# A two-layer hybrid encoder with a hierarchical mixture of experts: row gathers in two halves on 128 partitions

## The chip, the cores and the metric

The kernel runs on one core of a Trainium2 chip. The metric is the device time of one execution in microseconds; less is better. The core has a TensorE (matmuls and weight loads), a VectorE (DVE), a ScalarE (ACT), a GpSimd (POOL), a SyncE (SP), and 16 DMA engines that move data between DRAM and the on-chip memory (SBUF, 128 partitions). The matmuls write into PSUM.

## The reference

All numbers are fp32. 544 tokens (512 of a prompt and 32 of a running stream) of 1024 features pass through two layers. Each layer has a token mixer (A: sliding-window attention with sinks, B: differential attention), a residual add, and a mixture of experts. The change touches the mixture of experts, which reads, shortened:

```python
def hier_moe(h, ...):                      # h: rms_norm of the residual rows
    g_idx  = argmax(softmax(x @ w_rg + b_rg))          # 1 of 4 groups
    top_v, top_i = top_k(softmax(el of that group), 2) # 2 of its 8 experts
    gate   = g_prob * top_v / sum(top_v)               # 0 for all other experts
    for g in range(4):                                 # 32 experts in all
        a  = einsum('nd,edf->nef', x, w_gate[g])       # 1024 -> 256
        u  = einsum('nd,edf->nef', x, w_up[g])         # 1024 -> 256
        hh = silu(a) * u * gate[:, g, :, None]
        y  = y + einsum('nef,efd->nd', hh, w_down[g])  # 256 -> 1024
```

Each token goes to two of 32 experts. An expert has three matrices of 1 MB, so a layer reads 96 MB of expert weights.

## The kernel before

**Stages.** Layer 0's projections and attention are followed by its expert stage (about 256 to 494 us of the trace), then come layer 1's projections and attention, and its expert stage (about 893 to 1140). Tokens lie in five tiles (four of 128 rows, one of 32).

**Rows to experts.** After a tile's attention output is added, POOL writes the tile's residual rows to a scratch in DRAM, `hn_scratch`, one row of 4 KB per token (`rows_out`, L601). The router gives each token and choice an expert and a rank within it; an expert has `CAP` = 64 places. The rank of the token that stands in place s is a number in the constant table `C_SLOT`. A chain of matmuls against these tables makes, for each expert, a list that holds in place s the key of a token and choice; key = `KEY0` - 2 x token - choice. DVE turns keys into two lists of indices in `idx_i` (L1423 to L1426): the token, for the gather, and the half row of the output, for the scatter. The output scratch `y_scratch` (in the code `y2_dram`) holds 2 KB half rows, four per token: two choices by two halves.

**One expert.** In the profile a tensor `area` is the big SBUF buffer from which all tiles below are cut.

- POOL gathers (L667): an indirect DMA of up to 64 rows of 4 KB into `xg[e % 4]`. Even experts use partitions 0 to 63 and odd ones 64 to 127, each with 1024 columns.
- TensorE turns the rows (`x_transpose`, L2055): 8 transposes of 64 rows by 128 columns into one PSUM bank, so that features lie on partitions.
- DVE multiplies by the norm's gains on the way to SBUF (`scale_x`, L1463).
- TensorE multiplies by gate and up (`gate_up`, L2071 and L2072): 8 steps, each a pair that writes partitions 0 to 63 (gate) and 64 to 127 (up) of PSUM.
- ACT takes silu (L964), and DVE multiplies with up and the token's factor (L1469).
- TensorE transposes the result (`h_transpose`, L2077: two transposes of 64 by 128), DVE copies it (L1477), and TensorE multiplies by the down matrix (`down`, L2083 and L2084).
- DVE copies y (L1484), and POOL scatters 128 half rows of 2 KB (L673).

**Order.** TensorE's order is written out by hand: for each e, `gate_up(e)`, `x_transpose(e+1)`, `down(e-1)`, `h_transpose(e)`. POOL issues the first four gathers of a layer at once, and gather e+4 as soon as `x_transpose(e)` is done; scatters and gathers share its queue. SP issues the weight loads (L511) of 1 MB each in the order in which TensorE reads them (gate and up of e, then down of e-1) into 21 slots; a load waits for the last use of its slot. The down matrix is read as `(c p) d`: partition p holds rows p and 128 + p, two runs of 4 KB in DRAM. The gate and up matrices have one run of 8 KB per partition.

**A block beyond 64 rows.** When an expert has more than 64 rows, the rest goes through the same steps as an extra block after expert 21 (`overfull_rows`, with a chain of `STEPS` = 11 small DVE steps that makes its list in `ov_i`, and `overfull_expert` on TensorE). In layer 0 no expert has one; in layer 1 one expert with 72 rows does.

Late in the expert stage SP also reads the residual rows of four tiles back into `hid` (L550), whose space held weights meanwhile.

## Time and profile before

| | us |
|---|---|
| median of 3 runs | 1176.37 |
| lowest and highest of them | 1175.69, 1179.66 |
| profiled execution, its own time | 1176.92 |
| its span in the trace | 1175.0 |
| TensorE busy (PE) | 1037.6 |
| TensorE's weight loads (PEld, beside PE) | 738.9 |
| VectorE busy | 421.3 |
| GpSimd busy | 282.9 |
| ScalarE busy | 231.9 |

The profile's page divides the span into 40 slices of 29.4 us; each digit is a busy share in tenths, `PEclk` the granted TensorE clock in tenths of full speed, and `GB/s` what the 16 DMA engines moved. The expert stages are the two stretches at 370 to 403 GB/s (slices 10 to 17 and 32 to 39):

```
PE   6999999969999887939899899899999997999889970
PEclk9999999979999999959999999999997999999995
DMA  9312043559999999984320302145176999999996
GB/s 312 112 41 105 8 173 149 192 187 390 371 379 383 377 378 387 403 311 150 108 84 28 127 30 91 64 175 203 41 287 257 385 382 379 376 386 402 376 380 235
```

A busy TensorE is not one at its peak, and a matmul that waits for an operand is not counted as busy; a wait is put down to what came last.

### The profile page before, as it was taken

The page shows a single profiled execution, that of the slowest core. Times are in us where ns is not written, and L with a number is a line of the kernel's source. Part 1 is how long each engine was busy: PE and PEld are TensorE (multiplying, and loading weights), DVE is VectorE, ACT ScalarE, POOL GpSimd, SP SyncE. Part 2 cuts the span into 40 slices and gives each one's busy share as a digit, 9 for nine tenths or more (in the row PEclk, how much of TensorE's full clock was granted, in tenths as well). Part 3 has the DMA queues.
Part 4 walks back from the last instruction along what each step waited for, and adds up shares of the span by engine and source line. Part 5 has one row for each costly group of instructions (what it writes and reads, how often), then busy time and mean ns, then how long its engine had stood idle before and what let it go on. Part 6 is the DMA issues. An engine that isn't in the chain of part 4 may idle for free.

```text
span 1175.0 us, 18007 instructions
## 1 busy us (share of the span) xinstructions
PE 1037.6 (88%) x6864; PEld 738.9 (63%) x6864; DVE 421.3 (36%) x1365; ACT 231.9 (20%) x717; POOL 282.9 (24%) x440
## 2 busy tenths in 40 slices
PE   6999999969999887939899899999997999889970
PEld 6877778955555444528667687777884555555540
DVE  1234454333233222251242533435563333332326
ACT  4234441010000000023122333323310000000001
POOL 3612231022322222122021221221202223221213
PEclk9999999979999999959999999999997999999995
DMA  9312043559999999984320302145176999999996
GB/s 312 112 41 105 8 173 149 192 187 390 371 379 383 377 378 387 403 311 150 108 84 28 127 30 91 64 175 203 41 287 257 385 382 379 376 386 402 376 380 235
DMA packets 82168, 282.17 MB, mean 240 GB/s; under 512 B 10102, under 2 KB 36806, under 8 KB 64352
## 3 DMA queue, kind: packets, MB, share of 16 engines
q1 hardware_dynamic: 65840, 240.40, 54.7%
q0 software_dynamic: 14992, 31.66, 8.3%
q10 hardware_dynamic: 1248, 8.91, 2.0%
q8 instruction: 58, 0.95, 0.3%
q14 instruction: 30, 0.25, 0.1%
HBM read 268.66 MB, written 28.70 MB: 253 GB/s over the span
## 4 chain that ended last, share of the span: by engine, by line
PE 72%; DMA 15%; DVE 4%; SPq 3%; issue 2%; ACT 2%; POOL 1%; ACTq 0%; POOLq 0%; DVEq 0%
PE ps L1767 22%; PE ps L2071 14%; PE ps L1759 10%; DMA area<-in_w_up 9%; PE ps L2083 6%; PE ps L2055 4%; SPq L511 3%; DMA area<-in_w_down 3%; PE ps L2261 2%; PE ps L1743 2%; PE ps L1830 1%; PE ps L1952 1%; PE ps L2227 1%; PE ps L1967 1%; PE ps L1982 1%
## 5 line engine op out<-in xcount | busy, mean ns | idle before, releaser
L1767 PE MATMUL ps<-area 128*128 128x256 f32 x1152 | 267.8, 385 | 7.6 <-DMA area<-in_w_b_qkv 3.9
L2072 PE MATMUL ps<-area 128*64 128x256 f32 x1040 | 252.7, 399 | 0.0
L2071 PE MATMUL ps<-area 128*64 128x256 f32 x912 | 221.6, 399 | 30.2 <-DMA area<-in_w_up 20.3
L1767 PEld LDWEIGHTS ps<-area 128*128 128x128 f32 x1152 | 215.2, 192 | 38.7 <-issue 8.8
L2071 PEld LDWEIGHTS ps<-area 128*64 128x64 f32 x912 | 126.1, 143 | 92.7 <-issue 35.5
L673 POOL DMA_INDIRECT y_scratch<-area,idx_i x64 | 64.8, 1013 | 360.3 <-DVE area L1484 319.7
L2072 PEld LDWEIGHTS ps<-area 128*64 128x64 f32 x1040 | 143.4, 143 | 0.0
L1759 PE MATMUL ps<-area 128*128 128x272 f32 x512 | 123.2, 395 | 0.0
L1469 DVE SCALAR_TENSOR_TENSOR area<-ps,area 64x256 f32<-64x256 f32 x64 | 31.4, 491 | 246.2 <-ACT area L964 246.2
L964 ACT ACTIVATE area<-ps,area 64x256 f32<-64x256 f32 x64 | 29.9, 468 | 449.6 <-PE ps L2072 449.6
L2083 PE MATMUL ps<-area 128*64 128x512 f32 x228 | 109.9, 604 | 1.2 <-DVE area L1477 0.8
L2084 PE MATMUL ps<-area 128*64 128x512 f32 x228 | 109.9, 604 | 0.0
L1759 PEld LDWEIGHTS ps<-area 128*128 128x128 f32 x512 | 95.0, 190 | 18.9 <-issue 0.6
L929 ACT ACTIVATE area<-area,small 128x256 f32<-128x256 f32 (+5 forms) x160 | 80.2, 502 | 87.1 <-DVE small L1230 87.1
L2055 PEld LDWEIGHTS ps<-cst,area 64*128 64x128 f32 x512 | 61.3, 201 | 34.6 <-issue 29.3
L2055 PE MATMUL ps<-cst,area 64*128 64x64 f32 x512 | 70.1, 278 | 10.4 <-DMA area<-hn_scratch,idx_i 10.4
L1223 DVE CUSTOM_DVE_ANT_0 area<-ps,area 128x256 f32<-128x256 f32 (+5 forms) x160 | 59.1, 423 | 44.9 <-PE ps L1952 25.2
L667 POOL DMA_INDIRECT area<-hn_scratch,idx_i x64 | 61.3, 958 | 39.4 <-issue 19.9
L791 POOL TENSOR_SCALAR area<-area,small 32x288 f32<-32x288 f32 (+4 forms) x40 | 20.5, 521 | 162.0 <-DVE small L1655 162.0
L658 POOL TENSOR_SCALAR area<-area,small 128x256 f32<-128x256 f32 (+2 forms) x80 | 33.7, 439 | 92.5 <-DVE small L1258 92.5
L2083 PEld LDWEIGHTS ps<-area 128*64 128x64 f32 x228 | 26.7, 136 | 37.7 <-issue 32.4
L1477 DVE COPY area<-ps 128x128 f32<-128x128 f32 x64 | 18.6, 291 | 88.1 <-PE ps L2077 88.1
(235 smaller groups left out, 1157.1 us busy)
## 6 DMA issues: line engine op xcount, KB each, us to landing
area<-in_w_up SPq DMA_DIRECT2D x65, 1024.0 KB, 25.5
area<-in_w_gate SPq DMA_DIRECT2D x57, 1024.0 KB, 25.2
area<-in_w_down SPq DMA_DIRECT2D x57, 1024.0 KB, 25.6
area<-in_w_b_qkv SPq DMA_DIRECT2D x12, 1024.0 KB, 8.5
hid<-in_w_down SPq DMA_DIRECT2D x8, 1024.0 KB, 26.3
hid<-in_w_gate SPq DMA_DIRECT2D x8, 1024.0 KB, 26.6
area<-y_scratch ACTq DMA_DIRECT2D x8, 1024.0 KB, 8.1
area<-in_w_a_qkv SPq DMA_DIRECT2D x6, 1024.0 KB, 13.0
```

What stands on the lines that cost most here:

```text
L511: sp.dma_start(dst.rearrange("p (k f) -> p k f", f=src.shape[-1]), src).then_inc(landed, 16)
L667: nc.gpsimd.indirect_dma_start(xg[e % XG], None, hn_dram, bass.IndirectOffsetOnAxis(ap=idx_i[0:CAP, 1, e:e + 1], axis=0), bounds_check=N - ...
L673: nc.gpsimd.indirect_dma_start(y2_dram, bass.IndirectOffsetOnAxis(ap=idx_i[:, 0, e:e + 1], axis=0), yout[e % 2], None, bounds_check=4 * N ...
L929: ins = nc.scalar.activation(E[:r, g, 0:nk], E[:r, g, 0:nk], ACT.Exp, bias=sm[:r, 4 + g:5 + g], scale=SCALE, accum_out=sm[:r, 8 + g:9 + g])
L1223: ins = nc.vector.tensor_tensor_reduce(out=E[:r, g, 0:nk], in0=ps[:r, b, c:c + nk], in1=tab(j, g)[:r, tc:tc + nk], scale=1.0, scalar=-3e38 ...
L1759: ins = nc.tensor.matmul(ps[:, bank, 0:HALF_N], w[:, k, m * P:m * P + P], x[:, k, HALF_N * h:HALF_N * h + HALF_N], start=k == 0, stop=k == ...
L1767: ins = nc.tensor.matmul(ps[:r, bank, at_col:at_col + F], x[:, k, COL[t]:COL[t] + r], w[:, k, :], start=k == k0, stop=k == k1 - 1)
L2055: ins = nc.tensor.transpose(ps[:, 2 + b, k * CAP:k * CAP + CAP], x[:, k, :], ident[lo:lo + CAP, lo:lo + CAP])
L2071: nc.tensor.matmul(ps[0:CAP, bank, 0:F], x[:, k, :], wg[:, k, :], start=k == 0, stop=k == KD - 1)
L2072: ins = nc.tensor.matmul(ps[CAP:P, bank, 0:F], x[:, k, :], wu[:, k, :], start=k == 0, stop=k == KD - 1)
L2083: nc.tensor.matmul(ps[0:CAP, bank, :], ht[:, c, :], wd[:, c, 0:OUT_HALF], start=c == 0, stop=c == 1)
L2084: ins = nc.tensor.matmul(ps[CAP:P, bank, :], ht[:, c, :], wd[:, c, OUT_HALF:D], start=c == 0, stop=c == 1)
```

## The change

The edits, which belong together:

- `hn_scratch` becomes an array of 2 KB half rows like the output scratch, and each token's row stands in it twice, once for each of its two choices (`residual_rows`; `rows_out` writes both copies in one DMA of 1 MB per tile, and the read back of the residual takes the first).
- So one index, 4 x token + 2 x choice + half, serves gather and scatter. `C_HALF` now carries 2 x `KEY0` + half, and one DVE instruction makes the list in place of four. In the overfull block three chained steps fall away (`STEPS` 11 to 8).
- A gather takes 128 half rows of 2 KB: the first halves of the rows on partitions 0 to 63, the second halves on 64 to 127, into `xg` tiles of 512 columns.
- TensorE turns them by `turn_rows`: 4 x 2 x 2 = 16 matmuls of 64 by 64 against the identity in place of 8 transposes; the two of a pair read partitions 0 to 63 and 64 to 127 and write the same partitions of one PSUM bank.
- Feature 512 h + 8 c + k of a row thus lands on partition 64 h + c in step k, where it was before; gate and up weights and the gains are as they were.
- The down matrix is read as `(p c) d`, one run of 8 KB per partition, and `expert_ht` reads the gated rows with every second column to match.
- `C_SLOT`, the table of places: of the 64 places, counted s, s // 4 % 8 is a group of four partitions and s % 4 + 4 (s // 32) a turn; ranks go round the eight groups, one row to each, back and forth. Before, they went in quarters of 16.
- The y tile of the overfull block moves to make room.

```diff
--- before.py
+++ after.py
@@ -85,14 +85,14 @@
     c[:, C_K2:C_K2 + NT] = KEY0 - 2 * tok - 1
     c[:, C_BY1:C_BY1 + NT] = 1.0 / c[:, C_K1:C_K1 + NT]
     c[:, C_BY2:C_BY2 + NT] = 1.0 / c[:, C_K2:C_K2 + NT]
-    c[:, C_HALF] = np.arange(P) // CAP
+    c[:, C_HALF] = 2 * KEY0 + np.arange(P) // CAP
     c[:, C_THR:C_THR + 8] = CAP * np.arange(1, 9)
     c[:, C_IOTA:C_IOTA + NE] = np.arange(NE)
 
 
-    u, v, b = np.arange(CAP) // 16, np.arange(CAP) // 4 % 4, np.arange(CAP) % 4
-    quarter, at = (u + b) % 4, 4 * v + u
-    c[:, C_SLOT:C_SLOT + CAP] = 16 * quarter + np.where(quarter % 2 == 0, at, 15 - at)
+    s = np.arange(CAP)
+    group, turn = s // 4 % 8, s % 4 + 4 * (s // 32)
+    c[:, C_SLOT:C_SLOT + CAP] = 8 * turn + np.where(turn % 2 == 0, group, 7 - group)
     c[:, C_BEFORE:C_BEFORE + P] = np.arange(P)[:, None] < np.arange(P)[None, :]
     c[:, C_ONE:C_ONE + P] = 1.0
     q = np.arange(P)[:, None]
@@ -228,7 +228,7 @@
     def sem(name):
         return ctx.enter_context(nc.semaphore(name))
 
-    hn_dram = nc.dram_tensor("hn_scratch", [N, D], F32).ap()
+    hn_dram = nc.dram_tensor("hn_scratch", [4 * N, OUT_HALF], F32).ap()
     y2_dram = nc.dram_tensor("y2_scratch", [4 * N, OUT_HALF], F32).ap()
 
 
@@ -312,13 +312,13 @@
     junk = [part(norm_at[n] + 3 * D if n in norm_at else R_G, D) for n in range(5)]
 
 
-    xg = [part(D * (i // 2), D)[CAP * (i % 2):CAP * (i % 2) + CAP, :] for i in range(XG)]
-    xg_extra = part(R_G, D)[0:CAP, :]
+    xg = [part(OUT_HALF * i, OUT_HALF) for i in range(XG)]
+    xg_extra = part(R_G, OUT_HALF)
     M1 = XG // 2 * D
     xts = [part(M1 + 512 * i, KD, CAP) for i in range(2)]
     sil = [part(M1 + 1024 + 256 * i, F) for i in range(2)]
     hts = [part(M1 + 1536 + 128 * i, 2, CAP) for i in range(2)]
-    yout = [part(M1 + 1792 + 512 * i, OUT_HALF) for i in range(2)] + [part(R_G, OUT_HALF)]
+    yout = [part(M1 + 1792 + 512 * i, OUT_HALF) for i in range(2)] + [part(R_G + OUT_HALF, OUT_HALF)]
     assert M1 + 1792 + 2 * 512 <= slot_at["W0"] and slot_at["W0"] + SLOT <= M0
     ovw = part(R_R + 4 * SLOT, 3, SLOT)
     y2b = [part(2 * D * i, 2, D) for i in range(3)] + [part(R_X + 2 * D * i, 2, D) for i in range(2)]
@@ -347,7 +347,7 @@
     root = part(M0 + 3000, NE)
     assert M0 + 3000 + NE <= R_G
     first_of = sb("first_of", [P, NT, 2, 8], U32)
-    idx_i = sb("idx_i", [P, 3, NE], I32)
+    idx_i = sb("idx_i", [P, NE], I32)
     ov_i = sb("ov_i", [P, 8], I32)
     ov_u = sb("ov_u", [1, 8], U32)
 
@@ -481,6 +481,10 @@
 
         return at["ab"[layer], "o"], NT * (k_end // 2 - 1) + LATE.index(t) + 1
 
+    def residual_rows(t):
+
+        return hn_dram[4 * COL[t]:4 * COL[t] + 4 * ROWS[t], :].rearrange("(p c h) d -> p c (h d)", c=2, h=2)
+
     block = ctx.enter_context(nc.Block())
 
 
@@ -494,7 +498,7 @@
 
         gate = [I["w_gate"][l].rearrange("g e (p k) f -> (g e) p k f", k=KD) for l in range(2)]
         up = [I["w_up"][l].rearrange("g e (p k) f -> (g e) p k f", k=KD) for l in range(2)]
-        down = [I["w_down"][l].rearrange("g e (c p) d -> (g e) p c d", p=P) for l in range(2)]
+        down = [I["w_down"][l].rearrange("g e (p c) d -> (g e) p c d", p=P) for l in range(2)]
 
         def source(key):
             kind, x, i = key[0], key[1], key[2]
@@ -547,7 +551,7 @@
             for name in ("H1", "H0"):
                 sp.wait_ge(*last_use([key for key, at in MOE_LOADS[layer] if at == name][-1]))
                 for t in (2 * int(name[1]), 2 * int(name[1]) + 1):
-                    sp.dma_start(hid[:, t, :], hn_dram[COL[t]:COL[t] + P, :]).then_inc(tile_in[t], 16)
+                    sp.dma_start(hid[:, t, :], residual_rows(t)[:, 0, :]).then_inc(tile_in[t], 16)
 
             with sp.If(extra > 1):
                 with sp.Fori(1, extra) as o:
@@ -598,7 +602,7 @@
             t = TILES[n][i]
             r = ROWS[t]
             pool.wait_ge(hid_attn, OUT_DONE[n // 2][t])
-            pool.dma_start(hn_dram[COL[t]:COL[t] + r, :], hid[:r, t, :]).then_inc(y_out[i % 2], 16)
+            pool.dma_start(residual_rows(t), hid[:r, t, :].unsqueeze(1).broadcast_to([r, 2, D])).then_inc(y_out[i % 2], 16)
 
         def g_load():
             pool.dma_start(gbc, I["norm_final"].rearrange("(o d) -> o d", o=1).broadcast_to([P, D])).then_inc(g_in, 16)
@@ -665,20 +669,20 @@
 
             def gather(e):
                 nc.gpsimd.indirect_dma_start(xg[e % XG], None, hn_dram,
-                                             bass.IndirectOffsetOnAxis(ap=idx_i[0:CAP, 1, e:e + 1], axis=0),
-                                             bounds_check=N - 1, oob_is_err=False).then_inc(gath[e % XG], 16)
+                                             bass.IndirectOffsetOnAxis(ap=idx_i[:, e:e + 1], axis=0),
+                                             bounds_check=4 * N - 1, oob_is_err=False).then_inc(gath[e % XG], 16)
 
             def scatter(e):
                 wait_apart(pool, ye_sb, NE * layer + e + 1)
-                nc.gpsimd.indirect_dma_start(y2_dram, bass.IndirectOffsetOnAxis(ap=idx_i[:, 0, e:e + 1], axis=0),
+                nc.gpsimd.indirect_dma_start(y2_dram, bass.IndirectOffsetOnAxis(ap=idx_i[:, e:e + 1], axis=0),
                                              yout[e % 2], None, bounds_check=4 * N - 1, oob_is_err=False) \
                     .then_inc(scat[e % 2], 16)
 
             def overfull_gather(o, x):
                 wait_apart(pool, s["idx"], o + 1)
                 nc.gpsimd.indirect_dma_start(x, None, hn_dram,
-                                             bass.IndirectOffsetOnAxis(ap=ov_i[0:CAP, 4:5], axis=0),
-                                             bounds_check=N - 1, oob_is_err=False).then_inc(s["gath"], 16)
+                                             bass.IndirectOffsetOnAxis(ap=ov_i[:, 5:6], axis=0),
+                                             bounds_check=4 * N - 1, oob_is_err=False).then_inc(s["gath"], 16)
 
             def overfull_scatter(o):
                 wait_apart(pool, s["y"], o + 1)
@@ -689,10 +693,9 @@
             pool.wait_ge(at["ab"[layer], "o"], UNITS)
             for b in range(2):
                 pool.wait_ge(y_out[b], 16 * (3, 2)[b] * (layer + 1))
-            wait_apart(pool, r_idx, 2 * layer + 1)
+            wait_apart(pool, r_idx, layer + 1)
             for e in range(XG):
                 gather(e)
-            pool.wait_ge(r_idx, 2 * layer + 2)
             for e in range(NE):
                 if e + XG < NE:
                     wait_apart(pool, x_flip, NE * layer + e + 1)
@@ -1420,10 +1423,7 @@
 
             cnt = ovs[0:1, 0:NE]
             dve.wait_ge(r_slots, layer + 1)
-            own(dve, nc.vector.tensor_scalar(idx_i[:, 2, :], ps[:, 3, 0:NE], -1.0, float(KEY0), ALU.mult, ALU.add))
-            nc.vector.tensor_scalar(idx_i[:, 1, :], idx_i[:, 2, :], 1, None, ALU.arith_shift_right).then_inc(r_idx, 1)
-            own(dve, nc.vector.tensor_scalar(em[:, 0, :], ps[:, 3, 0:NE], -2.0, float(2 * KEY0), ALU.mult, ALU.add))
-            nc.vector.tensor_scalar(idx_i[:, 0, :], em[:, 0, :], cst[:, C_HALF:C_HALF + 1], None, ALU.add) \
+            nc.vector.tensor_scalar(idx_i[:, :], ps[:, 3, 0:NE], -2.0, cst[:, C_HALF:C_HALF + 1], ALU.mult, ALU.add) \
                 .then_inc(r_idx, 1)
 
             def per_tile(i):
@@ -1483,7 +1483,7 @@
                     dve.wait_ge(scat[b], 16 * (NE // 2 * layer + e // 2))
                 nc.vector.tensor_copy(yout[b], ps[:, 6 + b, :]).then_inc(ye_sb, 1)
 
-            STEPS = 11
+            STEPS = 8
             k = [0]
 
             def link(o, ins):
@@ -1529,10 +1529,7 @@
                 link(o, nc.vector.tensor_tensor_reduce(
                     out=blocks[:, 64:64 + NE], in0=ps[:, 3, NE:2 * NE], in1=blocks[:, 0:NE], scale=1.0, scalar=0.0,
                     op0=ALU.mult, op1=ALU.add, accum_out=ovs[:, 117:118]))
-                link(o, nc.vector.tensor_scalar(ov_i[:, 6:7], ovs[:, 115:116], -1.0, float(KEY0), ALU.mult, ALU.add))
-                link(o, nc.vector.tensor_scalar(ovs[:, 116:117], ovs[:, 115:116], -2.0, float(2 * KEY0), ALU.mult, ALU.add))
-                link(o, nc.vector.tensor_scalar(ov_i[:, 5:6], ovs[:, 116:117], cst[:, C_HALF:C_HALF + 1], None, ALU.add))
-                nc.vector.tensor_scalar(ov_i[:, 4:5], ov_i[:, 6:7], 1, None, ALU.arith_shift_right) \
+                nc.vector.tensor_scalar(ov_i[:, 5:6], ovs[:, 115:116], -2.0, cst[:, C_HALF:C_HALF + 1], ALU.mult, ALU.add) \
                     .then_inc(s["idx"], 1)
                 assert k[0] == STEPS, k
 
@@ -2049,12 +2046,16 @@
                     pe.wait_ge(s["count"], layer + 1)
                 if e >= 2 or layer:
                     wait_apart(pe, x_sb, NE * layer + e - 1)
-                x = xg[e % XG].rearrange("p (c k) -> p k c", k=KD)
-                lo = CAP * (e % 2)
+                turn_rows(xg[e % XG], 2 + b).then_inc(x_flip, 1)
+
+            def turn_rows(rows, bank):
+
+                x = rows.rearrange("p (c k) -> p k c", k=KD)
                 for k in range(KD):
-                    ins = nc.tensor.transpose(ps[:, 2 + b, k * CAP:k * CAP + CAP], x[:, k, :],
-                                              ident[lo:lo + CAP, lo:lo + CAP])
-                ins.then_inc(x_flip, 1)
+                    for lo in (0, CAP):
+                        ins = nc.tensor.matmul(ps[lo:lo + CAP, bank, k * CAP:k * CAP + CAP], x[lo:lo + CAP, k, :],
+                                               ident[lo:lo + CAP, lo:lo + CAP], start=True, stop=True)
+                return ins
 
             def gate_up(e):
 
@@ -2073,9 +2074,9 @@
                 return ins
 
             def expert_ht(h, bank):
+                rows = h[CAP:P, :].rearrange("s (p c) -> s c p", c=2)
                 for c in range(2):
-                    ins = nc.tensor.transpose(ps[:, bank, c * CAP:c * CAP + CAP], h[CAP:P, c * P:c * P + P],
-                                              ident[CAP:P, CAP:P])
+                    ins = nc.tensor.transpose(ps[:, bank, c * CAP:c * CAP + CAP], rows[:, c, :], ident[CAP:P, CAP:P])
                 return ins
 
             def expert_down(ht, wd, bank):
@@ -2116,10 +2117,7 @@
 
             def overfull_expert(o, rows):
                 wait_apart(pe, s["gath"], 16 * (o + 1))
-                x = rows.rearrange("p (c k) -> p k c", k=KD)
-                for k in range(KD):
-                    ins = nc.tensor.transpose(ps[:, 3, k * CAP:k * CAP + CAP], x[:, k, :], ident[0:CAP, 0:CAP])
-                ins.then_inc(s["xf"], 1)
+                turn_rows(rows, 3).then_inc(s["xf"], 1)
                 pe.wait_ge(s["xs"], o + 1)
                 pe.wait_ge(s["w"], 48 * (o + 1))
                 wv = ovw[:, :, :].rearrange("p j (k f) -> p j k f", f=F)
```

The order of the instructions on TensorE stays; in one expert's round, from the second half of `gate_up(e)` to the first of `gate_up(e+1)`, the turn has other instructions. Before, on TensorE, layer 0 (`cst` holds the identity; `...` leaves out the rest of `down`):

```order
L2072 MATMUL ps<-area 64x256
L2055 MATMUL ps<-cst,area 128x64 x8
L2083 MATMUL ps<-area 64x512
L2084 MATMUL ps<-area 64x512
...
L2077 MATMUL ps<-cst,area 128x64 x2
L2071 MATMUL ps<-area 64x256
```

The same place in the changed kernel, on TensorE:

```order
L2073 MATMUL ps<-area 64x256
L2056 MATMUL ps<-cst,area 64x64 x16
L2084 MATMUL ps<-area 64x512
L2085 MATMUL ps<-area 64x512
...
L2079 MATMUL ps<-cst,area 128x64 x2
L2072 MATMUL ps<-area 64x256
```

Nothing moved in its place: eight transposes of 128 by 64 became sixteen matmuls of 64 by 64, and the lines are one or two further down.

On POOL, at the end of a layer's attention and the start of its expert stage, before (the first two rows are small router steps, L601 is the write of a tile's rows, L667 a gather, L673 a scatter):

```order
L592 TENSOR_SCALAR small<-small 128x1
L593 TENSOR_TENSOR small<-small 128x1
L601 DMA hn_scratch<-hid 128x1024
L667 DMA area<-hn_scratch,idx_i 64x1024 x5
L673 DMA y_scratch<-area,idx_i 2176x512
L667 DMA area<-hn_scratch,idx_i 64x1024
```

And in the changed kernel, on POOL:

```order
L596 TENSOR_SCALAR small<-small 128x1
L597 TENSOR_TENSOR small<-small 128x1
L605 DMA hn_scratch<-hid 256x1x1024
L671 DMA area<-hn_scratch,idx_i 128x512 x5
L677 DMA y_scratch<-area,idx_i 2176x512
L671 DMA area<-hn_scratch,idx_i 128x512
```

Again nothing moved: the write has twice the rows and the gathers have 128 pieces of 512 columns.

## Rows read from the trace of the kernel before

**Rows 1.** Windows, layer 0's expert stage: us; busy PE, PEld, DVE, ACT, POOL; clock; DMA; GB/s

```profile
256.50:384.00 127.50, 126.11 (x930) 72.74 (x932) 37.29 (x72) 8.42 (x18) 33.94 (x36) 0.98 1.02 375
384.00:493.80 109.80, 90.30 (x626) 55.22 (x623) 26.93 (x52) 6.07 (x13) 23.18 (x24) 0.95 1.02 387
```

**Rows 2.** Chain of waits in that stage: start, duration, engine and line

```profile
265.88 0.43 PE ps L2071
...
303.36 1.03 PE ps L2055 x8
...
310.12 1.02 PE ps L2055 x8
...
493.75 0.40 PE ps L2071
```

**Rows 3.** Waits of TensorE, 256 to 505: total us, times, longest

```profile
PE ps L2071 <- DMA area<-in_w_up: 19.5, 12, 3.0
```

**Rows 4.** Windows of two us, and one after the last gather

```profile
353.00:355.00 2.00, 2.00 (x18) 1.05 (x16) 0.89 (x2) 0.00 (x0) 0.00 (x0) 1.00 0.99 408
355.00:357.00 2.00, 2.00 (x22) 1.35 (x20) 0.00 (x0) 0.00 (x0) 1.04 (x2) 1.00 1.06 307
...
360.00:362.00 2.00, 2.00 (x18) 1.22 (x18) 0.89 (x2) 0.00 (x0) 0.00 (x0) 1.00 1.04 424
362.00:364.00 2.00, 2.00 (x22) 1.19 (x18) 0.00 (x0) 0.00 (x0) 1.27 (x2) 1.00 1.04 309
...
476.00:490.00 14.00, 12.70 (x96) 7.85 (x93) 3.39 (x7) 0.78 (x2) 2.03 (x2) 1.00 1.02 413
```

**Rows 5.** POOL's timeline (start, duration), and DMA issues (median us to landing)

```profile
350.21 0.95 POOL L667 DMA_INDIRECT area<-hn_scratch,idx_i  x1 [0.30 <-issue]
...
area<-hn_scratch,idx_i POOLq DMA_INDIRECT x64, 7.7
```

**Rows 6.** DMA queues, 857 to 863, then 847 to 853: packets, MB, share

```profile
q1 hardware_dynamic: 413, 2.58, 102.4%
...
q0 software_dynamic: 167, 0.62, 25.6%
```

**Rows 7.** TensorE's timeline, then groups of weight loads by form (busy, mean ns)

```profile
86.91 1.09 PE L1967 MATMUL ps<-area 128*64 128x128 f32 x16
...
306.72 0.38 PE L2071 MATMUL ps<-hid,area 128*64 128x256 f32 x1
...
306.93 0.38 PE L2071 MATMUL ps<-hid,area 128*64 128x256 f32 x1
...
L2055 PEld LDWEIGHTS ps<-cst,area 64*128 64x128 f32 x512 | 61.3, 201 | 34.6 <-issue 29.3 <-DMA area<-hn_scratch,idx_i 5.3
L2077 PEld LDWEIGHTS ps<-cst,area 64*128 64x128 f32 x130 | 12.8, 137 | 52.5 <-issue 52.2 <-DVE area L1469 0.2
```

**Rows 8.** POOL's timeline ahead of layer 1's expert stage

```profile
875.48 0.60 POOL L601 DMA_DIRECT2D hn_scratch<-hid  x1 [20.08 <-DVE hid L1247]
...
887.40 1.24 POOL L667 DMA_INDIRECT area<-hn_scratch,idx_i  x1 [10.12 <-DVE idx_i L1426]
```

**Rows 9.** Layer 1's expert stage: TensorE's waits 980 to 1150, chain, window

```profile
PE ps L2071 <- DMA area<-in_w_up: 4.6, 3, 3.2
PE ps L2071 <- DMA area<-in_w_down: 2.5, 1, 2.5
PE ps L2071 <- DVE ov_i L1535: 2.4, 1, 2.4
...
1084.33 1.02 PE ps L2055 x8
...
1130.95 1.03 PE ps L2055 x8
...
1056.00:1062.00 6.00, 6.00 (x32) 3.50 (x31) 0.00 (x0) 0.00 (x0) 0.00 (x0) 0.58 1.03 394
```

## The prediction

> **What bounds the kernel now.** I read the windows first, then the waits of the expert stage, then the chain there, and last the DMA rate in pieces of two microseconds. The reader is to see which of two suppliers is late: TensorE, or the DMA that brings 3 MB of weights per expert. In layer 0's expert stage the DMA engines are busy all the time, at 375 and 387 GB/s [rows 1]. TensorE goes at its own pace at first: from one turn of gathered rows to the next it takes 6.76 us, 303.36 to 310.12 [rows 2]. Weights come in more slowly than that, the stock of 21 slots runs down, and the last third of the stage waits: 19.5 us in 12 waits, all for a weight load [rows 3]. So the last expert starts at 493.75. At TensorE's own pace it would start at 265.88 + 30 x 6.76 = 468.7 [rows 2]. This stage is bound by the DMA, with 25.05 us to be had before TensorE binds.
>
> Why is the DMA at 381 on average? It is not even. In each expert's 6.8 us there is a quiet part at 408 or 424 GB/s and a dip to 307 or 309; after the last gather there are no dips, and the rate is 413 with scatters still running [rows 4]. A gather issued at 350.21 lands 7.7 us later in the median, so at about 357.9: the dip of 355 to 357 is its data [rows 4, 5]. A scatter moves as many bytes, from 128 partitions, and lies in the quiet part. The gather writes into 64 partitions only. That is the difference on which I build.
>
> **The change part by part.** *Gathers over 128 partitions.* The same bytes arrive as 128 pieces of 2 KB instead of 64 of 4 KB. The sum: layer 0 moves 127.5 x 375 + 109.8 x 387 = 90.3 MB from 256.5 to 493.8 [rows 1]. At 413 GB/s, the rate without gathers [rows 4], that takes 218.6 us and ends at 475.1. The ends of this price: nothing (493.8, if the dips stay) and 424 GB/s (469.5). I take 413, because the scatter is the nearest row to the new gather: 2 KB pieces, 128 partitions, no dip.
>
> *The table of places* sets which partition a row falls into. It adds no instruction. Whether the 16 DMA engines get more equal shares no row shows; I take it at nothing, and the spread of the rate holds it.
>
> *Down weights by 8 KB runs.* One run per partition instead of two of 4 KB. Traffic that is mostly 8 KB pieces cost 102.4% of 16 engines for 6 us and 2.58 MB, 38.1 engine-us per MB; pieces of 4 KB alone 25.6% for 6 us and 0.62 MB, 39.6 [rows 6]. The difference of 1.5 on some 27 loads of 1.05 MB is 42 engine-us, over 16 engines 2.7 us a layer. The lower end is nothing. I take 2.7: the supply of layer 0 ends at 472.4.
>
> *TensorE turns the rows by 16 matmuls of 64x64 in place of 8 transposes of 64x128.* Eight transposes take 1.03 [rows 2]. An ordinary fp32 matmul stands in the trace as two passes, a transpose as one, so 16 matmuls are 32 passes, or 16 steps if the two halves of the array (the pairs at partitions 0 and 64) work at the same time. Pairs on two column halves do that: a pair step with 256 moving columns takes 306.93 - 306.72 = 0.21, and eight pair steps with 128 columns 1.09 in all, 0.13 or less each [rows 7]. With 64 columns I expect a quarter of the first, 0.054 (an estimate from these rows); 16 steps are then 0.86, with the start and the switch of shape about 1.0, the same as now. The ends: 0.86 and, at 0.13 a step, 2.1. I take no change, as the time went with the columns in both rows. If the halves go in turn it is a rival, below.
>
> *Transposes of the gated rows read every second column.* Loading a strided operand takes 201 ns and a dense one of the same size 137 [rows 7]. Two per expert: 0 to 0.13 us. I take 0.065, for the first of the two, since the second loads beside it. Over a layer that is 2.0 us of TensorE's pace, so layer 0's floor goes from 468.7 to 470.7. The DMA's 472.4 is later and decides: **layer 0 gains 493.75 - 472.4 = 21.3 us.**
>
> *Layer 1* has the same stage plus one block for an expert with more than 64 rows, and the DMA is nearly its equal, so TensorE's own work soon binds there. Six experts lie between the turns at 1084.33 and 1130.95: 46.62 us where 6 x 6.76 = 40.56 would do, so 6.1 goes with the weight waits [rows 9]. The block's weights are waited for 2.5 us; I count 1.6, because DVE must still scale the block's freshly turned rows [rows 9]. The block's list costs a wait of 2.4 on DVE, in which three of six chained steps fall away: 0.9 [rows 9]. After the wait for the block's weights its matmuls ran at a granted clock of 0.58, that is at the lower of the two levels for most of 6 us [rows 9]; if the wait goes, up to 2.6 us come back, and I count half. The strided transposes take 33 x 0.065 = 2.1. **Layer 1 gains 6.1 + 1.6 + 0.9 + 1.3 - 2.1 = 7.8 us.** With full clock it is 9.1, without it and without the block's terms 4.0.
>
> *Hidden edits.* The row scratch in DRAM is written twice, 1 MB per tile where it was 512 KB. 4 KB pieces cost 39.6 engine-us per MB [rows 6], so 1.3 us more for a tile. The last write of layer 1 is issued at 875.48 and the first gather waits until 887.40 for its list of indices [rows 8]: 11.9 us of cover. If it were gone, 1.3 us a layer. On POOL, which issues these writes, the gathers and the scatters in one queue, a gather costs 0.95 [rows 5]; even at twice that, one gather and one scatter fit in 6.76. DVE makes the indices in one instruction instead of four, ahead of the first gather: one of about 0.2 us goes from the path, which I do not count. Reading back the residual takes the same pieces at twice the step, in a part of the stage when its slots are no longer needed.
>
> **The sum.** 21.3 + 7.8 = 29.1. The profiled execution took 1176.92, 1.92 more than its span of 1175.0, and 0.55 above the median of 1176.37. 1176.92 - 29.1 = 1147.8; against the median **1147.3**.
>
> **The rivals.** *A, the two halves of the array go in turn.* Then a turn is 32 steps of about 0.055, 1.76, and with start about 0.8 above now. Layer 0's last expert starts at 265.88 + 0.8 + 30 x (6.76 + 0.065 + 0.8) = 495.4, 1.7 later than before, and TensorE binds from the first expert; layer 1 pays 33 x 0.865 = 28.5 and gets 9.9: 18.6 later. Together 20.3 slower: **1196.7**. It decides from 34.95 / 64 = 0.55 us per expert and turn on. For it speaks that no row shows two pairs that differ in rows and columns at once and write the same PSUM bank; against it, that pairs in two column halves do overlap [rows 7]. The Trainium skill, TensorEngine Tiling (Array Packing), section Restrictions and Gotchas, says that different row tiles cannot access the same PSUM bank simultaneously; the new pairs are different row tiles in one bank, on different partitions. No run here shows it yet; by that rule the time would be this rival's, by the rows above the forecast.
>
> *B, the dips belong to gathers as such* (their scattered reads), and spreading the destination changes nothing. Then 2.7 of layer 0 and about 1 of layer 1 remain: **1173**. Against it: the scatter is as scattered on the DRAM side and makes no dip [rows 4].
>
> *C, half of the dip stays.* The rate is 397, between 381 and 413: 90.3 / 397 = 227.5, the end 484.0 - 2.7 = 481.3, a gain of 12.4, and some 5 in layer 1: **1159**.
>
> **How the numbers follow.** The forecast has 0.64, with its own range of 1139 (full clock, 424 GB/s, a turn at 0.86) to 1155; C has 0.12, B 0.09, A 0.15. From 1139 to 1173 lie the forecast, C and B, 0.85 in all, and A is left out. About 0.3% is what a measurement of this kernel can tell from no change: 1172.8 to 1179.9. Faster by more: 0.64 + 0.12 and a little of B, 0.78; within: the rest of B, 0.07; slower: A, 0.15.
>
> **What would show it.** In the windows of the changed kernel the dips are gone and the stage runs at 410 GB/s or more; the turn's line on TensorE takes 1.0 per expert and the spacing stays near 6.8; the waits for weights shrink from 19.5 us in layer 0 to under 3; the last expert of layer 0 starts near 472. Spacing of 7.6 from the first expert on means A; dips of 300 GB/s mean B. The forecast is wrong if the turn costs over half a microsecond more, or if the DMA rate does not rise.

## The result: slower, and the profile after

The changed kernel takes 1217.16 us in the median of five runs (1215.6 to 1218.01), against 1176.93 for the kernel before in the same comparison: a ratio of 1.0335 with a 95% interval of 1.0319 to 1.0351. I had forecast 1147.3, in a range of 1139 to 1173. The profiled execution's span is 1215.0, against 1175.0 before.

The line of the page that shares the chain of work that ended last among the engines now reads, for the changed kernel:

```profile
PE 88%; DVE 4%; DMA 3%; issue 2%; ACT 2%; POOL 1%; ACTq 0%; SPq 0%; POOLq 0%; DVEq 0%
```

Before, the DMA had 15% of this chain, the weight loads above all. Now it has 3%, and TensorE is the bound nearly everywhere. The windows say why the DMA left the chain. Those of layer 0's expert stage in the changed kernel (columns as in [rows 1]), the whole stretch first, then pieces of two us:

```profile
256.50:384.00 127.50, 126.22 (x1190) 80.89 (x1186) 31.57 (x61) 7.48 (x16) 30.54 (x30) 0.97 1.01 411
...
344.00:346.00 2.00, 2.00 (x16) 0.81 (x14) 0.69 (x1) 0.00 (x0) 0.00 (x0) 1.00 0.98 409
346.00:348.00 2.00, 2.00 (x18) 1.24 (x18) 0.89 (x2) 0.00 (x0) 0.00 (x0) 1.00 1.04 413
348.00:350.00 2.00, 2.00 (x22) 1.28 (x18) 0.00 (x0) 0.00 (x0) 1.18 (x2) 1.00 1.02 422
350.00:352.00 2.00, 2.00 (x34) 1.76 (x30) 0.49 (x1) 0.47 (x1) 0.87 (x1) 1.00 1.03 422
```

The dips of [rows 4] are gone: over a whole round of 8 us no window falls under 409, and the stretch runs at 411 GB/s where [rows 1] has 375. What I built the forecast on has come true. TensorE's waits in that stage (256 to 520) are down to two rows, and neither is a weight load, where [rows 3] had 19.5 us of them:

```profile
PE ps L2072 <- DVE area L1463: 1.3, 2, 0.9
PE ps L2084 <- DVE area L1477: 0.4, 1, 0.4
```

And still the stage ends later. The chain there (start, duration) shows the price; L2056 is the turn of the rows, L2079 the transposes of the gated rows:

```profile
302.83 2.07 PE ps L2056 x32
...
306.77 0.38 PE ps L2079 x2
...
310.75 2.07 PE ps L2056 x32
```

A turn takes 2.07 where it took 1.03 [rows 2], and from turn to turn it is 7.92 where it was 6.76. No expert escapes that. TensorE's timeline gives the start of the first gate matmul for the last expert of layer 0, and for the first and the last expert of layer 1, in the changed kernel:

```profile
504.91 0.43 PE L2072 MATMUL ps<-area 128*64 128x256 f32 x1
...
905.09 0.69 PE L2072 MATMUL ps<-area 128*64 128x256 f32 x1 [0.84 <-DVE area L1463]
...
1174.61 0.43 PE L2072 MATMUL ps<-area 128*64 128x256 f32 x1
```

In the kernel before these were 493.75 [rows 2] and, in layer 1:

```profile
893.16 0.69 PE L2071 MATMUL ps<-area 128*64 128x256 f32 x1 [0.84 <-DVE area L1463]
...
1134.46 0.40 PE L2071 MATMUL ps<-area 128*64 128x256 f32 x1 [0.35 <-DMA area<-in_w_up]
```

So layer 0's expert stage lost 504.91 - 493.75 = 11.2 us. The part between the stages took 400.2 in place of 399.4. Layer 1's stage took 269.5 in place of 241.3, 28.2 more. Together 40.2, and the span grew by 40.0. The questions are why a turn costs 2.07, and what the DMA's gain is worth without that.

### The profile page after: what moved, and what is told of

Read it like the earlier page. It is cut to its first block, busy times and chain, and to the rows that moved or that the text cites. A ratio compares the mean times of both kernels' runs of the same rounds, so it can differ in the third digit from the quotient of the medians.

```text
span 1215.0 us, 21115 instructions
## 1 busy us (share of the span) xinstructions
PE 1105.6 (91%) x8424; PEld 803.0 (66%) x8424; DVE 420.0 (35%) x1356; ACT 232.0 (19%) x717; POOL 289.1 (24%) x440
## 3 DMA queue, kind: packets, MB, share of 16 engines
q8 instruction: 70, 1.15, 0.4%
## 4 chain that ended last, share of the span: by engine, by line
PE 88%; DVE 4%; DMA 3%; issue 2%; ACT 2%; POOL 1%; ACTq 0%; SPq 0%; POOLq 0%; DVEq 0%
PE ps L1764 21%; PE ps L2072 19%; PE ps L2056 11%; PE ps L2084 10%; PE ps L1756 10%; PE ps L2259 2%; PE ps L2079 2%; PE ps L1827 1%; PE ps L1740 1%; PE ps L1949 1%; PE ps L2225 1%; PE ps L1964 1%; PE ps L1979 1%; DMA area<-y_scratch 1%; PE ps L2073 1%
## 5 line engine op out<-in xcount | busy, mean ns | idle before, releaser
L2073 PE MATMUL ps<-area 128*64 128x256 f32 x1040 | 247.4, 393 | 0.0
L2072 PE MATMUL ps<-area 128*64 128x256 f32 x912 | 218.0, 394 | 7.3 <-DVE area L1463 3.3
L2072 PEld LDWEIGHTS ps<-area 128*64 128x64 f32 x912 | 124.3, 141 | 72.4 <-issue 11.3
L2056 PEld LDWEIGHTS ps<-cst,area 64*64 64x64 f32 x2080 | 129.9, 212 | 35.2 <-issue 30.1
L2056 PE MATMUL ps<-cst,area 64*64 64x64 f32 x2080 | 138.9, 284 | 10.9 <-DMA area<-hn_scratch,idx_i 9.8
L2073 PEld LDWEIGHTS ps<-area 128*64 128x64 f32 x1040 | 141.3, 141 | 1.4
L671 POOL DMA_INDIRECT area<-hn_scratch,idx_i x64 | 66.1, 1034 | 40.4 <-issue 37.7
L1463 DVE TENSOR_TENSOR area<-ps,gT 128x512 f32<-128x512 f32 x65 | 45.0, 692 | 76.7 <-PE ps L2056 76.7
L2079 PEld LDWEIGHTS ps<-cst,area 64*128 64x128 f32 x130 | 20.1, 202 | 52.1 <-issue 52.0
```

The source lines that it names most:

```text
L671: nc.gpsimd.indirect_dma_start(xg[e % XG], None, hn_dram, bass.IndirectOffsetOnAxis(ap=idx_i[:, e:e + 1], axis=0), bounds_check=4 * N - 1, ...
L1463: return nc.vector.tensor_tensor(x, ps[:, bank, :].rearrange("p (k c) -> p k c", c=CAP), gT[:, layer, :].unsqueeze(2).broadcast_to([P, KD, ...
L2056: ins = nc.tensor.matmul(ps[lo:lo + CAP, bank, k * CAP:k * CAP + CAP], x[lo:lo + CAP, k, :], ident[lo:lo + CAP, lo:lo + CAP], start=True, ...
L2072: nc.tensor.matmul(ps[0:CAP, bank, 0:F], x[:, k, :], wg[:, k, :], start=k == 0, stop=k == KD - 1)
L2073: ins = nc.tensor.matmul(ps[CAP:P, bank, 0:F], x[:, k, :], wu[:, k, :], start=k == 0, stop=k == KD - 1)
```

## The experiments

### What a step of the turn costs

The page counts 2080 matmul passes in 65 turns, 32 per turn, in pairs. I had priced a pair at 0.054 us, by its 64 moving columns; it took about 0.12. The first experiment adds turns of a resting weight tile behind TensorE's last work, in the changed kernel. Each sort stands twice in the sequence, on a line of its own. Two of the sorts:

```diff
+            for k in range(8):
+                for lo in (0, 64):
+                    nc.tensor.matmul(ps[lo:lo + 64, 2 + lo // 64, 64 * k:64 * k + 64], by8[lo:lo + 64, k, 0:64], ident[lo:lo + 64, lo:lo + 64], start=True, stop=True)
...
+            for k in range(8):
+                for lo in (0, 64):
+                    nc.tensor.matmul(ps[lo:lo + 64, 2 + lo // 64, 64 * k:64 * k + 64], row64[lo:lo + 64, k, 0:64], ident[lo:lo + 64, lo:lo + 64], start=True, stop=True)
```

`by8` reads every eighth column, as the turn of the change does, and `row64` neighbouring ones.

> The changed kernel, with idle turns of a weight tile added behind TensorE's last down matmuls; nobody reads them. Each sort stands twice, on a line of its own. Theory 1, the price of a step: two matmuls on the two halves of the array do overlap, and a pair takes 0.12 us whatever it moves, because a pass cannot be shorter than the loading of its strided operand. Theory 2, in turn: the two halves wait for each other, as they write one PSUM bank, and a matmul pass takes 0.06. Expected of 16 matmuls of 64x64 (32 passes), in us, theory 1 / theory 2: pairs in one bank as in the changed kernel 2.0 / 2.0; pairs in two banks 2.0 / 1.0; pairs with dense operands in one bank about 1.4 / 2.0; all 16 on one half of the array 3.8 / 2.0; first one half's eight, then the other's 3.8 / 2.0; pairs with 128 moving columns 2.0 to 2.2 / 3.4; pairs with 32 moving columns 2.0 / about 1.5. For other turns, theory 1 alone has numbers: eight transposes of 64x128 with strided operands 1.03 and dense ones 0.8; four transposes of 128x128 strided 0.55 and dense 0.5.

From TensorE's timeline, second time through. The length of a sort is the distance from its start to the next sort's, since the last duration of a row includes the drain:

```profile
1211.04 2.15 PE L2344 MATMUL ps<-cst,area 64*64 64x64 f32 x32
1212.96 1.52 PE L2347 MATMUL ps<-cst,area 64*64 64x64 f32 x32
1214.31 1.10 PE L2350 MATMUL ps<-cst,area 64*64 64x64 f32 x32
1215.24 4.00 PE L2353 MATMUL ps<-cst,area 64*64 64x64 f32 x32
1219.08 3.27 PE L2356 MATMUL ps<-cst,area 64*64 64x64 f32 x29
...
1225.21 1.09 PE L2361 MATMUL ps<-cst,area 64*128 64x64 f32 x8
1226.14 0.66 PE L2363 MATMUL ps<-cst,area 64*128 64x64 f32 x8
1226.73 0.75 PE L2365 MATMUL ps<-cst,area 128*128 128x128 f32 x4
1227.32 0.60 PE L2367 MATMUL ps<-cst,area 128*128 128x128 f32 x4
```

In order: strided pairs in two banks (L2344) 1.92; dense pairs in one bank (L2347) 1.35; dense pairs in two banks (L2350) 0.93; all 16 strided on one half of the array (L2353) 3.84; eight transposes of 64x128, strided 0.93 (L2361) and dense 0.59; four of 128x128, strided 0.59 (L2365) and dense 0.53. Strided pairs in one bank took 1.95, and with 32 moving columns in place of 64 as much. The dense transposes were cheaper than I expected.

One reading stands at once. All on one half costs 3.84, twice the 1.92 to 1.95 of the pairs (the second set has the pairs at 1.92 at full clock too), so the two halves do work at the same time, and theory 2 falls. Dense pairs in two banks take 0.93 / 16 = 0.058 per step, which is what I had priced; strided ones take 0.120.

The granted clock has to be read beside such rows, and here it was not the same for all (1.00 is the upper of its two levels, 0.50 the lower; a number between them is a mean over both). Windows of three of these sorts (the third number from the end is the clock):

```profile
1211.04:1212.96 1.92, 1.92 (x36) 1.92 (x36) 1.29 (x2) 1.15 (x2) 0.47 (x2) 0.50 0.00 0
1214.31:1215.24 0.93, 0.93 (x38) 0.93 (x35) 0.23 (x1) 0.00 (x0) 0.00 (x0) 1.00 0.26 88
1215.24:1219.08 3.84, 3.84 (x38) 3.84 (x35) 0.00 (x0) 0.00 (x0) 0.00 (x0) 1.00 0.34 137
```

The dense pairs in one bank ran at a mean of 0.67, so their 1.35 beside 0.93 at 1.00 says nothing about the bank. Nor do the pairs with 128 moving columns in this run, 3.18 at 0.67, and the ordering by halves, 2.95 at 0.77. A second set was to settle stride and bank.

> A second set of idle turns behind the last down matmuls of the changed kernel. From the first set: strided by 8, a pair pass took 0.12 in one bank or two; dense 0.084 in one bank and 0.058 in two. Theory 1: the strided operand sets the step, and its price goes with the step width or with the count of columns loaded; theory 2: sharing a bank sets it. In us for 16 matmuls (8 pairs), theory 1 / theory 2: stride 2 between the dense 1.35 and 1.95 or at the latter / 1.35 in one bank, and in two banks 1.9 / 0.93; stride 4 the same as stride 8 or a little under / 1.35; 32 loaded columns in place of 64, strided: 1.0 if the loaded columns are paid, 1.95 if a strided step has one price / 1.35. With 128 moving columns, dense, one bank 3.2 and two banks 1.7 (the column rate) if the bank is what made the first set's 3.18, and about 3.2 in both otherwise; strided in two banks 1.95. All 16 dense on one half of the array: 32 passes of 0.074 to 0.084, 2.4 to 2.7. Eight transposes of 64x128 with stride 2: 0.93 as with stride 8; four of 128x128 with stride 8: 0.59 as with stride 4.

Its second time through ran at a granted clock of 1.00; the first row below is a window of it up to 1214.60, and the rest has 1.00 too. The second row is the window of one sort, the pairs with stride 8 in one bank, the first time through. Then TensorE's timeline, second time through:

```profile
1202.18:1214.60 12.42, 12.42 (x257) 12.29 (x257) 7.31 (x6) 2.30 (x4) 4.16 (x5) 1.00 0.39 150
...
1187.96:1189.88 1.92, 1.92 (x38) 1.92 (x36) 0.77 (x1) 0.00 (x0) 0.00 (x0) 0.52 0.95 358
...
1202.18 1.18 PE L2342 MATMUL ps<-cst,area 64*64 64x64 f32 x32
1203.19 2.08 PE L2345 MATMUL ps<-cst,area 64*64 64x64 f32 x32
1205.11 2.08 PE L2348 MATMUL ps<-cst,area 64*64 64x64 f32 x32
1207.03 1.12 PE L2351 MATMUL ps<-cst,area 64*64 64x64 f32 x32
1208.08 1.21 PE L2354 MATMUL ps<-cst,area 64*32 64x64 f32 x32
1209.22 1.96 PE L2357 MATMUL ps<-cst,area 64*64 64x128 f32 x32
1211.02 1.91 PE L2360 MATMUL ps<-cst,area 64*64 64x128 f32 x32
1212.77 2.09 PE L2363 MATMUL ps<-cst,area 64*64 64x128 f32 x32
1214.68 2.02 PE L2365 MATMUL ps<-cst,area 64*64 64x64 f32 x32
1216.64 1.17 PE L2367 MATMUL ps<-cst,area 64*128 64x64 f32 x8
```

All at full clock, 16 matmuls:

| pairs | one bank | two banks |
|---|---|---|
| dense, 64 moving columns (first set) | | 0.93 |
| stride 2, 64 moving columns | 1.01 | 1.05 |
| stride 4 | 1.92 | |
| stride 8 | 1.92 | |
| stride 8, 32 loaded columns | 1.14 | |
| dense, 128 moving columns | 1.80 | 1.75 |
| stride 8, 128 moving columns | | 1.91 |

Outside the table, all 16 dense on one half of the array took 1.96 (L2365), under the 2.4 to 2.7 that I expected and about twice the 1.01 of the pairs with stride 2, so dense pairs overlap as well. Eight transposes of 64x128 took 1.01 at stride 2 (L2367) and 0.97 at stride 8, and four of 128x128 at stride 8 took 0.64.

Sharing a bank costs 0.05 at most in these rows, and with stride 2 nothing. The stride costs, from 4 columns on: 0.12 per step with 64 loaded columns, whether 64 or 128 columns move, and 0.071 with 32 loaded. So a step takes the longer of two: what the moving columns take (1.75 / 16 = 0.109 for 128, hence some 0.055 for 64), and what loading the strided operand takes. My expectation that stride 2 would be near stride 8 was wrong for these pairs.

The Trainium skill, TensorE: Matmul & The Clock Gate, section LDWEIGHTS (loading the stationary operand), gives the load's time by its column count alone, columns divided by 1.2 in ns; an estimate for 64 columns is 53 ns. The dense step of 58 ns lies near that, though by the reading above the moving columns set it; the strided one, 120 at the same count, does not, and there the measurement decides. The Trainium skill, TensorEngine Tiling (Array Packing), section Restrictions and Gotchas, has the rule that the prediction weighed as rival A, that different row tiles cannot access one PSUM bank at the same time. As a loss of time it would have made the pairs in one bank slower than in two; the rows at full clock have 1.01 against 1.05 and 1.80 against 1.75.

A third set was to price one half of the array alone, by loaded columns and stride.

> A third set of idle turns behind the last down matmuls of the changed kernel: what a pass costs on one half of the array by the number of loaded columns and by their stride, with 64 moving columns; eight matmuls (16 passes) each. If the loaded columns are paid at a stride of 8 (the 0.120 of 64 columns and the 0.071 of 32 in the second set): 128, 64 and 32 columns take 3.7, 1.9 and 1.1 us. If a widely strided pass has one price: 1.9 for all. Stride 4 as stride 8, stride 2 as dense. Dense, 64 moving columns set 0.061 per pass at 64 loaded columns: 1.0 for 64 and 32, and for 128 either 1.0 (loads hidden) or 2.0 (paid by column). Last, dense pairs of 16 matmuls in one bank and in two: 1.35 and 0.93 if sharing a bank costs what the first set showed; the same to 0.05 if that was the place in the sequence.

It fell nearly all into a stretch at a granted clock of 0.50. There, with 64 moving columns, dense passes took as much with 64 loaded columns as with 32 (1.89 and 1.84 for 16), which bears out that the moving columns set a dense step of 64. Passes of 128 loaded columns took 0.21 to 0.24, dense or by 2 or 4, too near each other to price those strides at full clock. The sort with 128 columns by 8 ran partly at 1.00:

```profile
1207.10 4.07 PE L2341 MATMUL ps<-cst,area 64*128 64x64 f32 x16
1211.09 2.18 PE L2343 MATMUL ps<-cst,area 64*64 64x64 f32 x16
```

That is 3.99 for 16 passes at a mean of 0.87, and 4.00 the first time through at 0.66: 0.249 per pass, twice the 0.120 of 64 columns. So at stride 8 the price goes with the count of loaded columns (0.071, 0.120 and 0.249 for 32, 64 and 128). The set answered its last question too: dense pairs in one bank took 1.76 at 0.50, where those of the first set took 1.35 at a mean of 0.67. That difference was the clock's, and not the bank's.

### The same price inside the kernel, and the supply without TensorE's brake

The dense turn, put into the changed kernel:

```diff
-                x = rows.rearrange("p (c k) -> p k c", k=KD)
+                x = rows.rearrange("p (k c) -> p k c", k=KD)
```

> The changed kernel with one edit: the sixteen matmuls of a turn read 64 neighbouring columns in place of every eighth one. The features then stand in another order than the weights', so the experts compute something else and layer 1 routes other rows; layer 0's expert stage has the same routing, the same instructions and the same DMAs, and only that stage is read. If the strided operand is the whole price: a turn takes about 1.05 in place of 2.07, the pace is 6.87 to 6.95, the DMA runs at 410 to 417 GB/s until the weights are in, and the last expert of layer 0 starts at 471 to 476, where the sum of the prediction had 472.4. If the shape or the shared bank costs something here that the idle turns did not show: a turn of 1.4 or more and a pace of 7.3 or more. If the supply is worse once TensorE runs ahead: dips, and a last start at 480 or later.

Of layer 0's expert stage in this kernel: two turns from the chain, the start of the last expert and what it followed, then the windows:

```profile
305.69 1.08 PE ps L2056 x32
...
312.62 1.08 PE ps L2056 x32
...
445.93 30.82 DMA area<-in_w_up
476.75 0.24 issue
476.99 0.40 PE ps L2072
...
256.50:384.00 127.50, 126.29 (x1350) 74.13 (x1348) 36.40 (x70) 8.41 (x18) 34.94 (x35) 0.97 1.01 410
384.00:460.00 76.00, 76.00 (x815) 44.01 (x813) 22.79 (x44) 5.14 (x11) 22.54 (x22) 1.00 1.02 416
```

The stride alone takes the turn from 2.07 to 1.08, and the pace from 7.92 to 6.93. With that the stage comes out where the prediction had it, nearly: the last expert starts at 476.99, a gain of 16.8 over 493.75, where the sum had 472.4 and 21.3, and a microsecond past the 471 to 476 expected here. The DMA is again the later supplier, at 416 GB/s, and 410 on average up to 384. In pieces of two us from 340 to 358 no window falls under 408, so the dips stay away at this pace too. Only this stage may be read; the stages behind it work on other rows.

### Which part of the change lifted the DMA's rate

Gathers with the pieces of the change, but into 64 partitions, and with the turn of before:

```diff
-                nc.gpsimd.indirect_dma_start(xg[e % XG], None, hn_dram,
-                                             bass.IndirectOffsetOnAxis(ap=idx_i[:, e:e + 1], axis=0),
+                for h in range(2):
+                    nc.gpsimd.indirect_dma_start(xg[e % XG][:, OUT_HALF * h:OUT_HALF * h + OUT_HALF], None, hn_dram,
+                                                 bass.IndirectOffsetOnAxis(ap=idx_i[0:CAP, h, e:e + 1], axis=0),
```

> The changed kernel with the gather alone put back on 64 partitions: two gathers of 64 pieces of 2 KB per expert (pieces as small as in the change) into the two column halves of 64 partitions, and the eight transposes of before. Table of places, down layout, scratch and index list are those of the change. If the 64 destination partitions make the dips: windows of layer 0's expert stage dip to about 310 GB/s again, the stage averages 380 to 385, and the time is 1172 to 1178, at most 3 us under before for the down layout. If the pieces' size, the table of places or the down layout removed the dips: 410 GB/s or more, no waits for weights in layer 0, and 1145 to 1152. In both cases a turn takes 1.03 us again.

It took 1179.83, a ratio of 1.0029 (1.0017 to 1.0041) to before, and 1.8 above the 1172 to 1178 that I expected; its last expert of layer 0 starts at 494.18. The windows of this kernel:

```profile
348.00:350.00 2.00, 2.00 (x18) 1.37 (x18) 0.89 (x2) 0.00 (x0) 0.00 (x0) 1.00 1.08 415
350.00:352.00 2.00, 2.00 (x22) 1.15 (x16) 0.00 (x0) 0.00 (x0) 1.31 (x2) 1.00 1.02 310
...
340.00:380.00 40.00, 40.00 (x296) 22.88 (x292) 11.43 (x23) 2.63 (x6) 16.59 (x18) 1.00 1.02 381
```

The dips are back, 310 beside 415, and TensorE waits 17.9 us for weights in layer 0. Pieces of 2 KB, the new table, the new scratch and the new down layout are all in this kernel. Beside the destination, two things differ from the change: a gather is split into two DMAs, and the turn is the old one. Neither made the dips: the kernel before has one DMA per gather and dips, and the dense turn has nearly the same pace (6.93, beside 6.87 here) and no dips. So the 64 destination partitions made them. It shows that, and not by what mechanism.

The down layout alone, in the kernel before:

```diff
-        down = [I["w_down"][l].rearrange("g e (c p) d -> (g e) p c d", p=P) for l in range(2)]
+        down = [I["w_down"][l].rearrange("g e (p c) d -> (g e) p c d", p=P) for l in range(2)]
```

with the transposes of the gated rows reading every second column, as in the change.

> The kernel before with one edit: the down matrices by one run of 8 KB per partition, and the gated rows read with every second column to match. By my terms the DMA gains 2.7 us in layer 0 and about 1 in layer 1, the transposes of the gated rows take 0.12 longer per expert (0.38 in place of 0.26, as in the changed kernel), which costs in layer 1 only: 1173 to 1176. If the size of the runs is worth nothing: 1176 to 1180. If it is what lifted the rate to 416 GB/s: 1150 or less.

It took 1175.12, a ratio of 0.9988 (0.9976 to 0.9999): a small gain, as summed. In the chain the last expert of layer 0 starts at 491.82, 1.9 earlier than before; I had put 2.7. The pace at the start of the stage is 6.87, 0.11 more than before, for the strided transposes.

The table of places was undone in the faster kernel of the next section, where the DMA is the bound in layer 0, so that a lower rate would show.

> The kernel with four transposes of 128x128, with the table of places of the kernel before and nothing else changed. I priced the table at nothing. If that holds: 410 GB/s in layer 0's expert stage, its last expert at 479, and 1145 to 1149, as with the new table. If the new table carries a part of the gain by evening out the 16 DMA engines' shares: a lower rate (395 to 405), the last expert of layer 0 later by 3 to 8 us, 1151 to 1160.

It took 1146.04 (ratio to before 0.9736, 0.972 to 0.9752), beside 1147.23 (0.9746, 0.973 to 0.9762) with the new table. The intervals overlap; the rates are 409 and 411 GB/s from 300 to 340 and from 420 to 460, against 409 and 410. The table is worth nothing that can be measured here.

### A turn that keeps the gain

Both halves of the rows now lie on all 128 partitions, so a transpose can take all of them at once, 128 columns at a time:

```diff
-                x = rows.rearrange("p (c k) -> p k c", k=KD)
-                for k in range(KD):
-                    for lo in (0, CAP):
-                        ins = nc.tensor.matmul(ps[lo:lo + CAP, bank, k * CAP:k * CAP + CAP], x[lo:lo + CAP, k, :],
-                                               ident[lo:lo + CAP, lo:lo + CAP], start=True, stop=True)
+                x = rows.rearrange("p (c k) -> p k c", k=KD // 2)
+                for k in range(KD // 2):
+                    ins = nc.tensor.transpose(ps[:, bank, k * P:k * P + P], x[:, k, :], ident)
...
-        gate = [I["w_gate"][l].rearrange("g e (p k) f -> (g e) p k f", k=KD) for l in range(2)]
+        gate = [I["w_gate"][l].rearrange("g e (h p k) f -> (g e) p h (k f)", h=2, p=P) for l in range(2)]
```

The up matrices and the gains follow the same order, and `scale_x` sorts the halves on its way out of PSUM. The price is that gate and up come in runs of 4 KB.

> The changed kernel with another turn: four transposes of 128x128, both halves of the rows at once, over all rows of the array. Features then lie by (half, partition, step), so gate and up come in two runs of 4 KB per partition in place of one of 8 KB. If the step's price is all that went wrong: the turn takes 0.5 to 0.6 us, TensorE's pace is 6.4 us per expert, layer 0's expert stage is bound by the DMA at 400 to 415 GB/s and its last expert starts at 470 to 478; layer 1 is bound by the DMA late or not at all: 1135 to 1150. If the supply is no better than before once TensorE stops holding it back (416 GB/s was only seen while slots were waited for by nobody): dips again, 1170 or more.

It took 1147.23, a ratio of 0.9746 (0.973 to 0.9762): faster than both kernels. From its chain, two turns and the start of layer 0's last expert:

```profile
343.01 0.68 PE ps L2059 x4
...
349.53 0.68 PE ps L2059 x4
...
457.07 21.89 DMA area<-in_w_up
478.96 0.24 issue
479.20 0.40 PE ps L2074
```

The turn takes 0.68, over the 0.5 to 0.6 that I expected, and the pace is 6.52. The DMA decides in layer 0, at 409 and 410 GB/s. The last start is 479.20, 2.2 later than with the dense turn and its 8 KB runs at 416. That the time equals my forecast is chance, since the sum behind it is another.

With the gated rows written in halves by ScalarE and VectorE, so that their transposes read dense columns:

```diff
-                nc.scalar.activation(sil[b][CAP:P, :], ps[0:CAP, b, 0:F], ACT.Silu, scale=root[0:CAP, e:e + 1]) \
+                nc.scalar.activation(sil[b][CAP:P, :].rearrange("s (c p) -> s c p", c=2), ps[0:CAP, b, 0:F].rearrange("s (p c) -> s c p", c=2), ACT.Silu, scale=root[0:CAP, e:e + 1]) \
...
-                nc.vector.scalar_tensor_tensor(sil[b][CAP:P, :], ps[CAP:P, b, 0:F], root[CAP:P, e:e + 1], sil[b][CAP:P, :],
+                h = sil[b][CAP:P, :].rearrange("s (c p) -> s c p", c=2)
+                nc.vector.scalar_tensor_tensor(h, ps[CAP:P, b, 0:F].rearrange("s (p c) -> s c p", c=2), root[CAP:P, e:e + 1], h,
```

> The kernel with four transposes of 128x128 and, on top, the gated rows written in halves (even features, odd features) by ScalarE and VectorE, so that the two transposes of the gated rows read dense columns. If the strided read is what made these two take 0.38 in place of 0.26: TensorE's pace falls from 6.53 to 6.41 per expert, layer 0 (bound by the DMA at the end) stays, layer 1 gains up to 33 x 0.12 = 4.0: 1143 to 1146. If the strided PSUM reads slow ScalarE and VectorE by more than that and they come onto the path: pace 6.5 or more, 1147 or more.

The time is 1146.32, a ratio of 0.9729 (0.9715 to 0.9744), no difference from the kernel above that the intervals allow and just over the 1143 to 1146 expected. The two transposes do go from 0.38 to 0.27 and the pace to 6.42, but in layer 1 the weights are now waited for at the end: 6.0 us in 4 waits for the up matrices, where the kernel above has 2.1 in one. What TensorE gives there, the DMA takes.

### What TensorE's time is worth in each stage

Two kernels do every turn twice into the same place, the kernel before and the one with four transposes; nothing else is changed:

```diff
-                for k in range(KD):
+                for k in (*range(KD), *range(KD)):
```

> The kernel before with each turn of rows done twice into the same place (eight transposes more per expert), so TensorE alone pays and no DMA is changed. 8 x 0.11 = 0.88 us more: a pace of 7.64. If each stage goes by its later supplier: layer 0's last expert starts at about 496 (TensorE's 265.9 + 30 x 7.64, against 493.75 that the DMA sets), 2 to 3 us lost; layer 1, where TensorE sets the end, pays 33 x 0.88 = 29 less the 6 of weight waits that it covers: 1199 to 1204. If TensorE's extra time hid beside the DMA in both layers, 1180 or less; if it were paid in full in both, 1233.

> The kernel with four transposes of 128x128, with each turn done twice (four more per expert, 4 x 0.15 = 0.6 us): a pace of 7.13. If each stage goes by its later supplier: layer 0's last expert at TensorE's pace starts at 267.5 + 30 x 7.13 = 481.4 against the DMA's 479.2, about 2 us lost; layer 1 pays 33 x 0.6 = 20 less the 4 or so of weight waits at its end: 1160 to 1167. If the DMA is the bound in both layers: 1150 or less.

The kernel before took 1201.33 with the doubled turn (ratio 1.0208, 1.0186 to 1.0229), 24 us more, at a pace of 7.65. Layer 0 waits for no weights any more, and its last expert starts at 497.07, 3.3 later than before. The kernel with four transposes took 1156.94 (0.9829, 0.9809 to 0.985), 9.7 more than with single turns and under my expectation, since four more transposes cost 0.48 and not 0.6 per turn (1.16 in place of 0.68). In it, layer 0's last expert stays where the DMA puts it:

```profile
456.30 22.22 DMA area<-in_w_up
478.52 0.24 issue
478.76 0.40 PE ps L2074
```

478.76, beside 479.20 with single turns: half a microsecond more per expert cost layer 0 nothing. Layer 1's stage, from the first expert's start to the last's, went from 227.8 to 236.9. That is the rule of the prediction, that each stage goes by its later supplier, on both sides of the point where it turns.

But layer 1 did not pay in full. The 9.1 are less than the 32 x 0.48 = 15.4 that the turns add there. Its last two rounds, which took 8.74 and 8.15 with waits for weights, take 7.01 each, and the round with the overfull block's matmuls, 10.57 at a granted clock of 0.84, takes 8.89 at 1.00. In the kernel before, layer 1's stage paid 16.7 of 32 x 0.89 = 28.5, where I had 23; the block's round went from 11.31 at 0.77 to 8.83 at 1.00. Another 3.5 came between the stages (402.9 in place of 399.4), of which 0.9 is layer 1's first turn and the rest was not looked into. So that total met the expectation by luck, and its parts did not.

## Why the prediction was wrong, point by point

**The DMA's part was right, and a little too high.** The dips belong to the 64 destination partitions (the gather back on 64 brings them back), the rate without them is 416 GB/s where I took 413, and the waits for weights are gone. Without the strided turn the last expert of layer 0 starts at 476.99, and I had 472.4. The sum's 90.3 MB by 472.4 amount to 418 GB/s from 256.5 on, as I took the down layout's 2.7 off on top of the rate of 413; that kernel moved 90.95 MB at 412 up to 477.0 (410 up to 384, and 416 behind). Rivals B and C fall with that: no dip is left.

**The step that failed is the price of the turn.** I wrote that 16 steps of 64 moving columns take 0.054 each, and that "the time went with the columns in both rows". Both rows, the gate step and L1967, have dense operands and many moving columns. The row of the operation that was being replaced spoke against it: eight transposes with 64 moving columns take 1.03 [rows 2], 0.13 each, more than twice what 64 columns cost by my rate. The moving columns did not set that row, so they could not be trusted to set its successor. Its group of weight loads even showed the slower strided load, 201 ns against 137 [rows 7], and I charged that to the gated rows alone. My upper end, 2.1 at 0.13 a step, was the nearest row, and the turn took 2.07: loading the strided operand set the step at 0.120, and with every column next to the other the same turn takes 1.08. I named the end and left it out of the cases. The sign that I named for being wrong, over half a microsecond more for the turn, came with 1.04.

**With that price the sum holds.** The turn costs 1.04 more per expert and the gated rows 0.11 (0.38 in place of 0.27), where I had 0 and 0.065: 6.76 + 1.15 = 7.91, and the pace is 7.92. Layer 0's second expert starts at 267.51, and 267.5 + 30 x 7.92 = 505.1 (measured 504.91). By the prediction's own count layer 1 pays 33 x 1.16 = 38.3 and gets the 9.9 of the four terms: 28.4. The sum would have been 1216 to 1217, and the kernel takes 1217.16.

**The four terms of layer 1 came out near, with some luck.** The stage lost 28.2 where this count gives 28.4, but only 32 turns lie between the two starts, 37.1, so 8.9 came back and not 9.9. The last four rounds, 6.5 over their pace before, now keep to it; I had 6.1. DVE's list is waited for 1.5 in place of 2.4, the 0.9 that I had. The two rounds at the block take 22.56 in place of 22.76, 2.5 less than the dearer turns would make of them; I had 1.6 + 1.3. The wait for the block's weights is gone, but the round of its matmuls still ran at a granted clock of 0.84, where it was 0.77. Against that, one round in the middle took 9.75, 1.8 over its pace, at a clock of 0.82.

**Rival A** had the sign and the chain of effects, TensorE binding from the first expert, with the wrong mechanism and half the price of a step. The halves do not go in turn: one half alone takes 3.84, pairs 1.92 to 1.95. It gave 1196.7 because it priced its 32 steps at 0.055, by moving columns again. The same error stood in the forecast and in the rival that should have guarded against it, so the range ended at 1173.

**The hidden edits** were hidden. The doubled write of the rows is 11.8 us ahead of layer 1's first gather in the changed kernel (886.80 and 898.61), as it was before [rows 8]. The table of places is worth nothing that shows, as taken. The down layout gave 1.9 us in layer 0 where I had 2.7.

**What stays open.** Why the strided load is dear from 4 columns on, and why a matmul's pass over 64 rows and 128 columns by 8 takes 0.249, while a transpose of the same operand takes 0.116 (0.93 / 8). The mechanism behind the 64 partitions wasn't tried.

## What to carry to other kernels

When an operation is replaced, price the new one first against the row of the one it replaces: if your rate does not reproduce the old row, the rate is not what sets it. Give the upper end that comes from such a row a case of its own, and make sure that the rival does not use the same rate as the forecast. And a stage with two suppliers 25 us apart, as layer 0's here, takes the first 25 us of added work of the earlier one for nothing and pays for the rest (36.2 were added, 11.2 lost), so ask of each edit how much it adds per turn of the loop before counting what it frees.

## What the runs showed of the hardware that I had not expected

- The price of a strided operand did not follow TensorE's clock: pairs with stride 8 in one bank took 1.92 at a mean granted clock of 0.52 and 1.92 at 1.00 (second set, first and second time through). Dense pairs did follow it: 1.76 at 0.50 (third set, one bank) and 0.93 at 1.00 (first set, two banks).
- It begins between a stride of 2 and 4 columns of 4 bytes: 1.01 for pairs at stride 2, 1.92 at 4 and at 8. For transposes of 64x128 it is there at stride 2 already (1.01, against 0.59 dense).
- Two matmuls on both halves of rows and columns overlap, in one PSUM bank as in two: 16 with 128 moving columns took 1.80 and 1.75, and 16 with 64 moving columns took 1.96 on one half and 1.01 as pairs with stride 2 in one bank.
- Four transposes of 128x128 turn as many elements as eight of 64x128 and take 0.68 in place of 1.03.
